# Four feed-forward stages of a float32 kernel: the down products of eight pairs as seven block products in place of eight

## The reference, cut to what matters

```python
def swiglu(h, w13, w2):
    g, u = jnp.split(h @ w13, 2, axis=-1)
    return ((jax.nn.silu(g) * u) @ w2).astype(h.dtype)
```

## Time and profile before

| | |
|---|---|
| median of 3 runs | 1630.48 us (1629.37 to 1631.04) |
| span of the profiled execution | 1629.7 us |
| TensorE busy | 1620.2 us, 99% |
| VectorE busy | 1027.7 us, 63% |
| ScalarE busy | 809.7 us, 50% |
| GpSimd busy | 70.9 us, 4% |
| transfers | 294.80 MB, mean 181 GB/s |

### The profile page before, as it was taken

The page is one execution under the profiler, slowest core; times in us unless marked ns, Lnnn a source line. Parts: engine busy times, 40 slices in busy tenths (PEclk is TensorE's granted clock), DMA queues, the critical chain, the costliest instruction groups (busy, mean ns, idle before and its releaser), DMA issues.

```text
span 1629.7 us, 22153 instructions
## 1 busy us (share of the span) xinstructions
PE 1620.2 (99%) x9216; PEld 1396.8 (86%) x9217; DVE 1027.7 (63%) x1110; ACT 809.7 (50%) x1003; POOL 70.9 (4%) x83
## 2 busy tenths in 40 slices
PE   9999999999999999999999999999999999999999
PEld 7998888889888887888888888888888887788887
DVE  6687555574665557555587655566664577765655
ACT  6445544455554446444554444455443455854443
POOL 0233000000000000000000000000100011000000
PEclk9999999999999999999999999999999999999999
DMA  8535658564455564565565655557545652065562
GB/s 288 162 114 163 220 170 243 181 219 156 155 194 181 179 205 157 189 225 176 186 219 165 212 179 196 192 169 239 186 157 201 211 185 79 24 209 182 169 206 90
DMA packets 221493, 294.80 MB, mean 181 GB/s; under 512 B 7644, under 2 KB 185264, under 8 KB 221394
## 3 DMA queue, kind: packets, MB, share of 16 engines
q1 hardware_dynamic: 215786, 284.33, 52.6%
q10 hardware_dynamic: 5608, 9.06, 2.1%
HBM read 290.75 MB, written 1.57 MB: 179 GB/s over the span
## 4 chain that ended last, share of the span: by engine, by line
PE 95%; DVE 3%; ACT 1%; DMA 1%; issue 0%; POOL 0%; SPq 0%; ACTq 0%; POOLq 0%; DVEq 0%
PE ps L2108 28%; PE ps L2274 21%; PE ps L2112 15%; PE ps L2147 3%; PE ps L2136 3%; PE ps L2138 3%; PE ps L2099 2%; PE ps L2096 2%; PE ps L2097 2%; PE ps L2204 2%; PE ps L2206 2%; PE ps L2205 2%; PE ps L2195 1%; PE ps L2398 1%; PE ps L2480 1%; PE ps L2490 1%
## 5 line engine op out<-in xcount | busy, mean ns | idle before, releaser
L1341 DVE TENSOR_TENSOR wlo<-raw,whi 128x2048 fp32r<-128x2048 f32 (+1 forms) x279 | 600.6, 2168 | 271.4 <-ACT whi L701 270.3
L701 ACT ACTIVATE whi<-raw 128x2048 fp32r<-128x2048 f32 x263 | 494.5, 1900 | 51.7 <-DMA raw<-in_ffn_w_down 12.7
L2108 PE MATMUL ps<-x_both,whi 128*128 128x512 f32 x2080 | 497.0, 391 | 0.0
L2108 PEld LDWEIGHTS ps<-x_both,whi 128*128 128x128 f32 x2080 | 385.1, 188 | 76.6
L2112 PEld LDWEIGHTS ps<-x_both,wlo 128*128 128x128 f32 x2080 | 267.5, 191 | 10.6
L2112 PE MATMUL ps<-x_both,wlo 128*128 128x256 f32 x2080 | 270.7, 283 | 0.0
L2274 PE MATMUL ps<-whi,hhi 128*128 128x512 f32 x480 | 188.1, 392 | 0.0
L2274 PE MATMUL ps<-wlo,hhi 128*128 128x512 f32 x480 | 187.4, 390 | 0.0
L2274 PE MATMUL ps<-whi,hlo 128*128 128x512 f32 x480 | 186.8, 389 | 0.0
L818 ACT ACTIVATE hid<-ps 128x512 f32<-128x512 f32 x54 | 32.2, 597 | 193.0 <-PE ps L2112 193.0
L1519 DVE TENSOR_TENSOR hid<-ps,hid 128x512 f32<-128x512 f32 x54 | 37.3, 691 | 133.7 <-ACT hid L818 133.7
(11 more groups left out here) (287 smaller groups left out, 1703.8 us busy)
## 6 DMA issues: line engine op xcount, KB each, us to landing
raw<-in_ffn_w_gate_up SPq DMA_DIRECT2D x80, 1024.0 KB, 5.2
raw<-in_ffn_w SPq DMA_DIRECT2D x62, 1024.0 KB, 5.2
raw<-in_ffn_w_down SPq DMA_DIRECT2D x44, 1024.0 KB, 5.0
raw<-in_hgrn_w_in SPq DMA_DIRECT2D x14, 1024.0 KB, 6.1
raw<-in_moba_w_in SPq DMA_DIRECT2D x12, 1024.0 KB, 5.2
raw<-in_conv_w_in SPq DMA_DIRECT2D x10, 1024.0 KB, 5.1
raw<-in_ffn_w_gate_up SPq DMA_DIRECT2D x16, 512.0 KB, 4.9
raw<-in_kv_w SPq DMA_DIRECT2D x6, 1024.0 KB, 5.1
```

What stands on the lines that cost most here:

```text
L701: act.activation(whi[s % WRING][:, 0:width], raw[n % RING][:, 0:width], ACT.Copy).then_inc(split_hi, 1)
L1341: ins = dve.tensor_tensor(wlo[s % WRING][:, part], raw[n % RING][:, part], whi[s % WRING][:, part].bitcast(F32), ALU.subtract)
L2108: pe.matmul(ps[:, bank + n, :], hi[:, k, n * P:(n + 1) * P], x_both[:, k], start=k == 0, stop=k == KT - 1, skip_group_check=True)
```

## The change

It concerns ffn1, ffn2, ffn3 and ffn5. Pairs 0 to 3 and pairs 4 to 7 form two blocks b = 0, 1. A block's part of the down product is a matrix product of hid (256 tokens x 1024 hidden) with 1024 x 1024 weights. Both are cut in 2 x 2 blocks (A: tokens x hidden, 128 x 512 each; B: hidden x columns, 512 x 512 each), and instead of eight block products seven are made, of sums and differences (the Winograd form of Strassen's scheme). Pairs 8 to 10 stay as they were.

- **TensorE**: a product is 4 k x 3 = 12 matmuls of 512 columns (`product`). Order: g1 u1 g2 u2 g3 u3, then g4 p(0,0) u4 p(0,1), g5 p(0,2) u5 p(0,3), g6 p(0,4) u6 p(0,5), g7 p(0,6) u7, g8 p(1,0) u8 p(1,1), g9 p(1,2) u9 p(1,3), g10 p(1,4) u10 p(1,5) p(1,6), d8 d9 d10. The seven are called A11, A12, S1, S2, S3, A22, S4 by their left side.
- **Weights**: the four quarters of a block are loaded by SyncE straight into four areas of the arena, beside the ring (`load_quarter`), at g2, u2, g3, u3 for block 0 and u6, g7, g8, u8 for block 1. VectorE makes four sums of 128 x 2048 (`weight_sum`): after the step of u2, g3, u3, u4 for block 0, after p(0,6), u7, g8, u8 for block 1. Each of the seven right sides is split in high and low as any chunk.
- **Left sides**: the multiply writes hid into a space for a whole block. GpSimd makes S1 to S4 (`blocks`), four sums of 128 x 512 on two operands in SBUF, as soon as the block's last multiply is done. ScalarE and VectorE make the high and low part (`left_high`, `left_low`), two items ahead of the product, behind the split of the item three ahead; two buffers.
- **Results**: a product lies in one bank; VectorE adds it to h at once (`drain`), 14 times a stage, the product S3 to two halves of h at a time. Three products share bank 0 and two bank 3, each added up on what is there, so a later one waits for the drain of the earlier one.
- The stage's end (`finish_stage`) keeps its four adds. Some small tensors move into the arena to make room.

```diff
+PRODUCTS = 7
+P_A11, P_A12, P_S1, P_S2, P_S3, P_A22, P_S4 = range(PRODUCTS)
+PRODUCT_BANK = (0, 2, 3, 0, 0, 1, 3)
+PRODUCT_STARTS = (P_A11, P_A12, P_S1, P_A22)
+LAST_LOADS = {("u", 6): 1, ("g", 7): 0, ("g", 8): 3, ("u", 8): 2}
+FIRST_LOADS = {("g", 2): 1, ("u", 2): 2, ("g", 3): 0, ("u", 3): 3}
+WEIGHT_SUMS = {("u", 2): (0, 0), ("g", 3): (0, 1), ("u", 3): (0, 2), ("u", 4): (0, 3),
+               ("p", 0, 6): (1, 0), ("u", 7): (1, 1), ("g", 8): (1, 2), ("u", 8): (1, 3)}
...
+        product_src = [r_area[r] for r in (0, 3, 1, 0, 4, 3, 2)]
+        left_src = [a11, a12, s_area[0], s_area[1], s_area[2], a22, s_area[3]]
...
             def ffn(name):
...
+                    for i in range(1, PAIRS):
+                        load(columns(up, i * CW), name, "g", i)
+                        load_quarter(name, "g", i)
+                        load(columns(up, F_FF + i * CW), name, "u", i)
+                        load_quarter(name, "u", i)
...
+            def ffn_blocked(name):
...
+                for k in range(LAST_UP):
+                    item, before, later = ORDER[k], ORDER[k - 1] if k else None, ORDER[k + 2]
...
+                    split_item(ORDER[k + 3])
+                    if k and before[0] == "g":
+                        gate_silu(before[1])
+                    if later[0] == "p":
+                        left_high(*later[1:])
+                    if item[0] == "g":
+                        gate_low(item[1])
+                    if item[0] == "u":
+                        up_low(item[1])
...
+                    pool.tensor_tensor(s1, a21, a22, ALU.add).then_inc(s_ready, 1)
...
+                    pool.tensor_tensor(s2, s1, a11, ALU.subtract).then_inc(s_ready, 1)
...
+                    pool.tensor_tensor(s3, a11, a21, ALU.subtract).then_inc(s_ready, 1)
...
+                    pool.tensor_tensor(s4, a12, s2, ALU.subtract).then_inc(s_ready, 1)
...
+                    if i >= BLOCK_PAIRS:
+                        n = first_block(name) + i // BLOCK_PAIRS - 1
+                        dve.wait_ge(s_ready, 4 * n + (3 if i % BLOCK_PAIRS < 2 else 4))
+                    dve.tensor_tensor(hid_slot(i), hid[:], silu[:], ALU.mult).then_inc(hid_ready, 1)
...
+                        ins = dve.tensor_tensor(t3, b22, b12, ALU.subtract)
...
+                        ins = dve.tensor_tensor(b12, b12, b11, ALU.subtract)
...
+                        ins = dve.tensor_tensor(b11, t3, b11, ALU.add)
...
+                        ins = dve.tensor_tensor(b21, b21, b11, ALU.subtract)
...
+                for k in range(LAST_UP):
+                    item, later = ORDER[k], ORDER[k + 2]
+                    split_item(ORDER[k + 3])
+                    if later[0] == "p":
+                        left_low(*later[1:])
+                    if item[0] == "g":
+                        sum_gate(item[1])
+                    if item[0] == "u":
+                        multiply(item[1])
+                    if item[0] == "p":
+                        drain(*item[1:])
+                    if name == "ffn2" and item in (("u", 2), ("u", 3)):
+                        final_norm(item[1] - 2)
+                    if item in WEIGHT_SUMS:
+                        weight_sum(*WEIGHT_SUMS[item])
+                split(name, "d", STANDARD)
+                left_low(1, P_S4)
+                last_multiply(0)
+                last_multiply(1)
+                last_low(0)
+                last_low(1)
+                drain(1, P_A22)
+                hid_low(STANDARD)
+                split(name, "d", STANDARD + 1, parts=(0,))
+                drain(1, P_S4)
+                hid_low(STANDARD + 1)
...
+                def product(b, j):
...
+                    pe.wait_ge(a_low, u + 1)
+                    for k in range(4):
+                        for m, (a, w_part) in enumerate(((high, hi), (high, lo), (low, hi))):
+                            mm = pe.matmul(ps[:, PRODUCT_BANK[j], :], a[:, k, :], w_part[:, k, :], start=j in PRODUCT_STARTS and k == 0 and m == 0,
+                                           stop=k == 3 and m == 2, skip_group_check=True)
```

More of the change, by code:

```diff
@@ L159, in plan @@
                     self.add(name, "og", i)
+            elif name in BLOCKED:
+                self.add(name, "first", 0, transfers=2)
+                self.add(name, "first", 1, transfers=2)
+                for item in ORDER:
+                    self.add(name, *item, made=item[0] == "p")
             elif name.startswith("ffn"):
@@ L373, in build @@
         hlo_ready = sem("hlo_ready")
+        r_landed = [sem(f"r_landed{r}") for r in range(4)]
+        t_done = sem("t_done")
+        s_ready = sem("s_ready")
+        a_high = sem("a_high")
+        a_low = sem("a_low")
+        p_drained = sem("p_drained")
+        hid0_kept = sem("hid0_kept")
         const_landed = sem("const_landed")
@@ L595, in ffn @@
                     load(pair[:, 4 * n:4 * n + 4, :, 0:CW], name, "first", n)
+                if name in BLOCKED:
+                    for i in range(1, PAIRS):
[3 more added lines that the diff above has]
+                        load_quarter(name, "u", i)
+                    for i in range(STANDARD, PAIRS):
+                        load(down_rows(down, i * CW), name, "d", i)
+                    return
                 load(columns(up, CW), name, "g", 1)
@@ L807, in activate, with ffn @@
+            def ffn(name):
+                if name in BLOCKED:
+                    ffn_blocked(name)
+                    return
+                base = FFNS.index(name) * (PAIRS + 2)
+                sums = FFNS.index(name) * (PAIRS - 1)
+                lows = parts_before(name)
                 def activate(i):
@@ L851, in ffn @@
                         activate(i)
-                    if name == "ffn2" and i == 5:
-                        for t in range(TT):
-                            act.wait_ge(h_ready[t], 2 * updates("ffn2"))
-                        load_gains(PHASES.index(name) + 3)
                     if name == "ffn0" and i == 3:
@@ L1530, in last_low, with left_low @@
                 def last_low(n):
[L1531 removed]
+                    dve.wait_ge(hhi_ready, lasts + 1 + n)
                     dve.tensor_tensor(xlo[:, n, :], hid[:, n, :], xhi[:, n, :].bitcast(F32), ALU.subtract).then_inc(hlo_ready, 1)
[L1534 to L1536 removed]
+                def left_low(b, j):
+                    u = uses + PRODUCTS * b + j
+                    dve.wait_ge(a_high, u + 1)
+                    high, low = left(u)
+                    dve.tensor_tensor(low, left_src[j], high.bitcast(F32), ALU.subtract).then_inc(a_low, 1)
@@ L2331, in ffn @@
                 across_pair(6, name, "u", 1)
-                for i in range(PAIRS - 2):
+                for item in ORDER[2:LAST_UP] if blocked else ():
+                    if item[0] == "g":
+                        pe.wait_ge(gate_summed, summed + item[1] - 1)
+                        across_pair(4, name, *item)
+                    elif item[0] == "u":
+                        pe.wait_ge(hid_ready, ups + 1 + item[1])
+                        across_pair(6, name, *item)
+                    else:
+                        product(*item[1:])
+                for i in () if blocked else range(PAIRS - 2):
                     if i >= 1:
```

482 lines of the change are left out of this document (387 added, 95 removed).

## The result

The changed kernel takes 1654.16 us in the median (1653.02 to 1654.94), the kernel before 1630.53 us on the same chip: a ratio of 1.0145 (95% interval 1.0131 to 1.0159). The change makes the kernel 1.4% slower, 23.6 us. Forecast was 1643.4 us with a range to 1653: the sign holds, the size does not. The profiled execution has a span of 1653.1 us, 23.4 us more than the one of before. In the kernel after, the products are L2725 (in `product`), the first product of pair 8 to 10 is L2691, the splits on VectorE are L1607 (from the ring) and L1617 (for a product), the left low part L1824, the weight sums L1841 to L1850, GpSimd's sums L1529 to L1540.

The account below looks back on a forecast made before the run. TensorE was taken to bound the kernel, busy 99% of the span. Saving 21.9 us and adding 34.8 us of stalls gave +12.9 us on 1629.7, plus 0.8: 1643.4 us, range 1617 to 1653, the forecast's own 1634 to 1652.

Parts of the forecast that it names:

- The saving: TensorE, four stages: seven block products for eight, 96 matmuls of 512 columns fewer at 0.228 us, 21.9 us off.
- Sum: Stalls of 8.1 us in three stages and 10.5 in ffn2, 34.8 together; less 21.9 saved, +12.9 us.
- Granted clock below 1.00 in a stage after a stall: Listed among the signs that would show the forecast wrong; no size given.
- Place 1: Second block, end of g7 to product (1, A12): no slack, GpSimd's four sums make 3.5 us of stall.
- (1, S1): Next left low part after (1, A12): VectorE needs 9.2 us, TensorE 8.3, so 0.9 us stall.
- Place 2: First block: (0, A12) late by 1.35 us, next product 1.35; in ffn2 4.2 and 0.9 us.
- The end of a stage: Between u10 and pair 8: VectorE and ScalarE need 6.5 us, TensorE has 5.47, so 1.0 us stall.
- The turns: GpSimd and VectorE alternate on two SBUF operands: each 128x512 GpSimd sum holds a VectorE split up 1.09 us.
- turns are not taken: Rival, 22%: GpSimd's sums run beside VectorE's splits without holding them up; 10.2 us of stalls, 1618.8 us.
- nothing stalls: Rival, 5%: VectorE's 88% load fits in all stages and the whole saving comes; 1608.6 us.
- partly covered: Rival, 10%: VectorE's waits overlap better by 0.1 us an item, some 2 us a stage go; 1635 us.
- The early transfers are later: Rival, 8%: 1 MB takes 3.3 us, g4 lands 2.2 us later, place 2 costs 2.5 more a stage; 1653 us.

Follow-up runs that it names:

- e3: The changed kernel with VectorE's eight weight sums a stage cut from 128x2048 to 128x16 elements, S3 fed with the weights of b22: 1613.6 us.
- e2: The changed kernel with matmuls of zeros filling TensorE's stalls in front of products (0, A12), (0, S1) and (1, A12): 1646.4 us.
- e11: All work kept but reordered to leave little stall; against that version, product (1, A12) made to wait for 24 small GpSimd steps: 1639.8 us, 24.1 us more.
- e1: The changed kernel with each of GpSimd's left-side sums cut from 128x512 to 128x4 elements: 1619.8 us.
- e7: First block's weight quarters loaded two ring loads earlier, against a version with later weight sums, final norm's steps and pair 8's high part earlier: 1634.1 us.
- e10: The changed kernel with the left side's four sums a block made by VectorE in place of GpSimd, spread over four steps: 1646.0 us.
- e4: The changed kernel with the third and fourth weight sum of each block made later on VectorE, all work kept: 1627.2 us, median of ten executions.

## Why the prediction was wrong in size

**The saving** (21.9 us): right. 96 matmuls fewer at 0.228 us, and e3, which has nearly no stalls, stands 16.3 us below the kernel before: 21.9 less 3.4 us at the ends of the stages and 2 us.

**The sum's missing term is the clock.** The step that failed is "Sum": it counts a stall at its own length and lets TensorE go on at 0.228 us a matmul behind it. "Granted clock below 1.00 in a stage after a stall" stood among the things that would show the forecast wrong, with no price; it happened at six stalls. Its net price in this kernel is 7.7 us by e2, some 1.3 us for each of the six. (e11, another kernel, has 7.7 us for four longer stalls, 1.9 us each.) With the stalls filled the kernel takes 1646.4 us, 3 us from the forecast's 1643.4 and inside its own range. So the working for VectorE's queue held, and the clock put the time beyond the range. VectorE's work grew by 49.2 us a stage (a quarter of 1224.4 less 1027.7), for the forecast's 44.7 and the lengthening by GpSimd.

**Place 1, (1, A12)**: forecast 3.5 us, all from GpSimd's turns, measured 3.50 us by the wait and 3.7 by the distance of starts, in four of four stages (the 5.1 us in the waits are ffn2's (0, A12)). e1 takes it to nothing; so does e3, which gives VectorE slack. **(1, S1)**: forecast 0.9 us, absent in the kernel after, 0.7 us in e2: the slow clock in front of it hid it.

**Place 2** was under-sized. In ffn1 (0, A12) and (0, S1) are late by 1.8 and 1.3 us for 1.35 and 1.35, in ffn3 and ffn5 (0, A12) by 2.4 and 2.2, in ffn2 by 5.3 for 4.2. Two terms are seen. From the end of ScalarE's part of g4 to the product it is 25.6 us in ffn1, ffn3 and ffn5 alike, for the forecast's 23.0 + 2.5, so the walk along VectorE's queue was right; what differs is when g4 landed. In ffn1 ScalarE had it by 483.1 us, 23.7 us after g1's start in place of 22.9, for the quarters fill the line of transfers:

```profile
481.15 1.92 ACT L829 ACTIVATE whi<-raw 128x2048 fp32r<-128x2048 f32 x1 [4.04 <-DMA raw<-in_ffn_w]
```

And in ffn2 the norm's second step stands beside GpSimd's first sum and is held up too, which the sum priced at 1.41 us:

```profile
690.42 2.46 DVE L1675 SCALAR_TENSOR_TENSOR h<-h,rstd_final,gain 128x512 f32<-128x512 f32 x2
```

**The end of a stage**: forecast 1.0 us, measured 0.84 (0.7 by the waits). All stalls together: forecast 34.8, measured 32.1, and with what the slow clock hid (e2's four waits in front of (1, S1) and the one in front of (0, S1), 4.7 us by the distance of starts) some 37 us.

**The turns.** The forecast took 1.09 us a sum from one collision, gave "turns are not taken" 22%, and was right to prefer the row. The Trainium skill's page SBUF — State Buffer, Who interferes with whom, says that a VectorE instruction with two inputs in SBUF contends with a GpSimd instruction that reads SBUF, and calls the port pair that they share an exclusive lock. The rows agree on both sides (3.38 us for 2.29, and GpSimd's own sum 3.28 us for 1.56). The other rivals: "nothing stalls" and "partly covered" are refuted by the waits. "The early transfers are later" had the right time, 1653 us, for the wrong reason, so its nearness is luck: g4's transfer was 0.8 us later than the forecast's in ffn1, not 2.2, and e7 shows what transfers cost when they really are in the way.

**The chances** had 58% on slower, which came true; the range ended at 1653 since every term in it was a length of VectorE's queue or of the line of transfers. No bound was drawn for a stall's consequence.

## What to carry to other kernels

When TensorE is the bound, a stall put into it can cost more than its length, by the clock: here 1.3 us net for each of six stalls in the kernel after and nearly 2 us for each of four in e11. Filling the stalls with matmuls of zeros brought 7.7 us back (e2); whether several short waits are cheaper than a long one was not tested. Work handed to an engine that is 88% busy has to be placed by its queue: the same steps cost 24 us or gained 15 us, by where they stand. Sums on GpSimd are not free beside VectorE's two-operand steps; one of 128x512 costs VectorE more (some 1.1 us, by 3.39 for 2.29) than doing it itself (0.69 us), as long as VectorE has no slack, and nothing where it has.

## What the hardware showed unexpectedly

How long TensorE idled does not settle whether its clock falls. It fell behind stalls of 3.7 us (four of four in the kernel after), 5.3 us (its ffn2), 5.1 (four of four in e11), 2.4 us (ffn3 of the kernel after), and behind three of e10's eight stalls of 2.0 us, but not behind the other five, nor behind 2.2 us in ffn5 of the kernel after, 2.8 us in ffn2 of e10 or 3.1 us in ffn2 of e4's profiled execution. Nor is a stall of that length needed: in e10 the clock also fell, for 6.8 us, 2.5 us after a wait of 0.9 us outside the four stages, where TensorE had turned to small matmuls (128 x 60), and in the kernel before it fell for 3.4 us in a mixer whose longest wait nearby is 0.7 us. And three of e4's ten executions lost time to the clock that the other seven did not. A fall lasted 3.4 or 6.8 us. What decides between them is open.

In e1 GpSimd's first sum of 128x4 in a block took 2.16 us in the median (L1529), the third and fourth 0.21 us (L1536, L1540). The first began at 560.36 us in ffn1, while VectorE's weight sum ran from 560.20 to 562.48, and ended at 562.55: it waited for VectorE's running step, however small it is itself, so its size tells little of its duration. The four large ones take 13.1 us in the second block of ffn1.
